# Sample attention scores of a hybrid decoder step: key blocks ordered across four batches, products in four column groups, eight key buffers of two pages

## The chip, the cores and the metric

The kernel runs on one NeuronCore of one Trainium2 chip. The core has five engines with their own instruction streams: PE (matrix products and transposes), DVE (vector work), ACT (scalar functions and copies), POOL (here it issues DMAs) and SP (it only issues DMAs). Sixteen DMA engines move the data. The metric is the device time of one execution in microseconds (us); less is better.

## The reference, cut to what matters

One inference step of a decoder layer for a prompt (512 tokens) and a sample group (8 batches of 4 new tokens, 2048 past positions each in a paged cache of 128 rows a page). The change concerns the attention of the sample group alone. Each batch has its own sixteen pages, named by a page table that is only known at run time:

```python
a_all = jnp.concatenate([gather_pages(cache_a), P['a_rows']], axis=1)      # head group A: k_cmp, v_cmp, k_slc, v_slc, two kv heads
w_all = jnp.concatenate([win_buf, P['win_rows']], axis=1)                  # the last 512 rows: window keys and values
...
s_s = jnp.einsum('bktgd,bktnsd->bktgns', qt, k_s) * scale + bias           # selected blocks (the kernel scores all keys, then masks)
s_w = jnp.einsum('btkgd,bskd->btkgs', qg, kw) * scale + pair_bias(rel_w)   # window
...
s = jnp.einsum('bthd,btkd->bthk', q, k_g) * HEAD_DIM ** -0.5 + bias        # head group C: one kv head, 256 best of 2048 keys
p = masked_softmax(s, ...);  o = jnp.einsum('bthk,btkd->bthd', p, v_g)
```

All of it is float32.

## The kernel before

The program is a chain of five phases; each begins when PE, ACT and DVE have all ended the one before. Phase 4 is the sample attention, phase 5 the output projection. Everything below is phase 4.

**Units and steps.** There are three units: u = 0 (head group A, batches 0 to 3), u = 1 (group A, batches 4 to 7) and u = 2 (group C, all eight batches). In a unit each batch owns 32 of the 128 rows of the scores. `STEPS` (L642) gives the order on every engine: head 0, body 0, head 1, turn 0, body 1, head 2, turn 1, body 2, turn 2. A *head* scores the first eight blocks of a unit (for u < 2 the window keys), a *body* the others (32 blocks for u = 0 and 1, 24 for u = 2), a *turn* transposes the softmax output so that it can multiply the values.

**A block.** PE transposes four 128x128 key tiles into PSUM bank 5 or 6 (`kb`, L1652, transposes on L1660), ACT copies the bank to one of four buffers `kT` (`take_k`, L790), and PE multiplies it with 32 query columns (`kmm`, L1664, product on L1673): 512 score columns in the 32 rows of that batch. A block of units 0 and 1 is four pages of one kv head; so each load of four pages (512 KB) feeds two blocks. A block of unit 2 is four pages of 64 KB. Batches come one after the other: all blocks of batch 0, then of batch 1. The product of a block stands behind the transposes of the next.

**Key loads.** SP walks the loads in the same order (`keys`, L1004) into four buffers `kn` of four pages; a load waits until the buffer's former blocks are transposed (`kb_tr`). A page number is taken from registers: `page` (L682) reads the sixteen page numbers of a batch with one load from the page table tile `ptab` (L684, an instruction TENSOR_LOAD in the trace), and only when the batch differs from the last one (`held`). A few register operations (L686) and one DMA a page follow.

**Value loads.** `values(eng, page, m)` fills one of four buffers `vr`: m = 0 to 15 are half batches of group A (8 pages of 128 KB), m = 16 to 23 the eight batches of group C (16 pages of 64 KB). A load waits until the product four before it is done (`pv_b`). POOL issues m = 0 to 15 and the odd ones of 16 to 23; SP issues the even ones of 16 to 23 behind its last key load.

**Value products.** `pv(u, x)` (L1686, products on L1682) works on batch x // 2 of the former unit and is put into the body of the next one, every 5 blocks (body 1) or 4 blocks (body 2). It already uses four column groups. The fifth call in body 2, `pv(1, 4)`, stands behind the 20th of the 24 blocks, and its two halves free the buffers for m = 16 and 17. Turn 2 ends with the eight products of unit 2, one for each of m = 16 to 23.

**Between the steps.** DVE adds biases and finds the maximum in `late` (L844) when a body's scores are done; the next head's scores wait for it (`un_s`), since they go to the same banks. In bodies 0 and 1 DVE also works off rounds of a top-k over 2080 columns, ahead of `late`. Body 0 starts when `early` (L806) has read the window scores of head 0, for which twelve bias loads must be in.

Of the kernel before, what the change touches and what calls it, by code (L numbers as in the profile page):

```python
# [38 lines left out]
P = 128  # L39
# [4 lines left out]
DB, DT = 8, 4  # L44
# [4 lines left out]
NPG = PAST // PAGE  # L49
NPOOL = 5 * DB * NPG // 4  # L50
HD = 128
AH, KVH, G = 8, 2, 4
# [12 lines left out]
NKR, NVR = 4, 4  # L65
# [125 lines left out]
def build(nc, I, O):  # L191
# [3 lines left out]
    with ExitStack() as ctx:  # L195
# [139 lines left out]
        keep, _ = region(apos[0] + 6 * 1024)  # L335
# [42 lines left out]
        kn = [at_(f"kn{i}", P, 1024) for i in range(NKR)]  # L378
        kT = [at_(f"kT{i}", P, 512) for i in range(4)]
# [9 lines left out]
        assert tpos[0] <= apos[0] + 6 * 1024  # L389
# [110 lines left out]
        vh_in = [sem(f"vh_in{i}") for i in range(2)]  # L500
        kk_in = [sem(f"kk_in{i}") for i in range(NKR)]
# [113 lines left out]
        sblocks, kloads = [], []  # L615
# [12 lines left out]
        kkneed, kc_ = [], [0] * NKR  # L628
        for m, (k_, _, _) in enumerate(kloads):
            kc_[m % NKR] += 16 * k_  # L630
            kkneed.append(kc_[m % NKR])
        vneed, vc_ = [], [0] * NVR
        for m in range(24):
            if m < 16 or m % 2:
                vc_[m % NVR] += 16 * (8 if m < 16 else 16)
                vneed.append((vr_in[m % NVR], vc_[m % NVR]))
            else:
                vneed.append((vh_in[m % NVR // 2], 16 * NPG * (m // 4 - 3)))
# [61 lines left out]
        def values(eng, page, m):  # L700
# [3 lines left out]
            slot, s = vr[m % NVR], vneed[m][0]  # L704
# [85 lines left out]
        def take_k(eng, copy, n, gt, s):  # L790

            eng.wait_ge(kb_tr, gt + 1)
            if n >= 4:
                eng.wait_ge(kb_mm, 32 + n - 3)
            copy(kT[n % 4][:, :], bank[5 + gt % 2][:, :]).then_inc(s, 1)  # L795
# [99 lines left out]
        def _(sp):  # L895
# [108 lines left out]
            def keys(step, u):  # L1004
                for m, (_, last, (lu, kind, b, q)) in enumerate(kloads):
                    if last not in blocks_of(step, u):
                        continue
                    if m >= NKR:
                        sp.wait_ge(kb_tr, kb_gt[kloads[m - NKR][1]] + 1)
                    slot, s = kn[m % NKR], kk_in[m % NKR]  # L1010
                    if kind == "win":
                        sp.dma_start(v3(slot, "p (i c) -> p i c", c=256), sw[b, :, 0, :, :].rearrange("(i p) h c -> p i (h c)", p=P)).then_inc(s, 16)
                    for i in range(4 if kind != "win" else 0):
                        r = page(b, 4 * q + i)
                        if kind == "slc":
                            sp.dma_start(slot[:, i * 256:(i + 1) * 256], ca[bass.ds(r, 1), :, 2, :, :].rearrange("a p h c -> (a p) (h c)")).then_inc(s, 16)
                        else:
# [14 lines left out]
            for m in range(16, 24, 2):  # L1032
                values(sp, page, m)
# [18 lines left out]
        def _(pool):  # L1052
# [110 lines left out]
            for m in [*range(16), *range(17, 24, 2)]:  # L1163
                values(pool, page, m)
# [10 lines left out]
        def _(pe):  # L1175
# [476 lines left out]
            def kb(n):  # L1652

                nonlocal gt
                u, kind, b, q, k, m = sblocks[n]
                pe.wait_ge(kk_in[m % NKR], kkneed[m])
                kturn(gt)
                w = 256 if u < 2 else P
# [65 lines left out]
            for step, u in STEPS:  # L1724
# [997 lines left out]
```

## Time and profile before

| what | value |
|---|---|
| median of 3 runs | 2112.82 us (2109.31 to 2113.4) |
| the profiled execution: its own time | 2106.33 us |
| its span, first to last instruction | 2104.6 us |
| PE, DVE, ACT, POOL busy | 1905.7, 939.8, 563.4, 183.4 us |
| the scores' transposes (L1660) and products (L1673) on PE | 79.5 and 124.9 us |

The span is what the profiler saw between the first and the last instruction; the time lies 1.7 us around it. Busy times of matrix products overlap a little in the trace, since products are pipelined; the distance between two starts is the better price. Phase 4 lies between about 1562 and 1879 us of the span.

### The profile page before, as it was taken

The page shows a single profiled execution, that of the slowest core. Times are in us where ns is not written, and L with a number is a line of the kernel's source. Part 1 is how long each engine was busy: PE and PEld are TensorE (multiplying, and loading weights), DVE is VectorE, ACT ScalarE, POOL GpSimd, SP SyncE. Part 2 cuts the span into 40 slices and gives each one's busy share as a digit, 9 for nine tenths or more (in the row PEclk, how much of TensorE's full clock was granted, in tenths as well). Part 3 has the DMA queues.
Part 4 walks back from the last instruction along what each step waited for, and adds up shares of the span by engine and source line. Part 5 has one row for each costly group of instructions (what it writes and reads, how often), then busy time and mean ns, then how long its engine had stood idle before and what let it go on. Part 6 is the DMA issues. An engine that isn't in the chain of part 4 may idle for free.

```text
span 2104.6 us, 36109 instructions
## 1 busy us (share of the span) xinstructions
PE 1905.7 (91%) x14415; PEld 1620.3 (77%) x14415; DVE 939.8 (45%) x1799; ACT 563.4 (27%) x1117; POOL 183.4 (9%) x338
## 2 busy tenths in 40 slices
PE   5999999999989989578999999889978798869997
PEld 3899999999978878457999999667743333349997
DVE  3122223122442566213888774648758472123331
ACT  2223233124332222123222222034433332231110
POOL 1000000000000001000000000100021043430000
PEclk9999999999989999779999999869999899859999
DMA  8986687724123312243533333650026466672331
GB/s 249 291 223 181 187 241 208 206 90 125 45 66 99 97 59 80 71 130 108 183 110 81 81 102 96 222 186 1 1 80 210 140 218 206 195 218 79 123 123 43
DMA packets 305426, 286.99 MB, mean 136 GB/s; under 512 B 40613, under 2 KB 291990, under 8 KB 303581
## 3 DMA queue, kind: packets, MB, share of 16 engines
q1 hardware_dynamic: 288555, 229.22, 37.6%
q0 software_dynamic: 16704, 55.48, 8.0%
q8 instruction: 114, 1.87, 0.4%
q14 instruction: 53, 0.43, 0.1%
HBM read 268.28 MB, written 29.14 MB: 141 GB/s over the span
## 4 chain that ended last, share of the span: by engine, by line
PE 82%; DMA 4%; DVE 4%; SPq 4%; issue 3%; ACT 1%; ACTq 0%; POOL 0%; POOLq 0%; DVEq 0%
PE bank L1484 6%; PE bank L1486 6%; PE bank L1485 6%; PE bank L1275 6%; PE bank L1277 6%; PE bank L1276 6%; PE bank L1673 5%; PE bank L1809 3%; PE bank L1811 3%; PE bank L1810 3%; PE bank L1525 3%; PE bank L1660 3%; PE bank L1257 3%; PE bank L1526 3%; PE bank L1527 2%
## 5 line engine op out<-in xcount | busy, mean ns | idle before, releaser
L1484 PE MATMUL bank<-h_lo,hw_hi 128*128 128x272 f32 x1024 | 308.4, 301 | 7.6 <-DVE vN L2435 6.7
L1486 PE MATMUL bank<-h_hi,hw_hi 128*128 128x272 f32 x1024 | 298.9, 292 | 0.0
L1485 PE MATMUL bank<-h_hi,hw_lo 128*128 128x272 f32 x1024 | 297.6, 291 | 0.0
L1275 PE MATMUL bank<-w1hi,xl 128*127 128x256 f32 x1024 | 296.5, 290 | 0.0
L1277 PE MATMUL bank<-w1hi,xh 128*127 128x256 f32 x1024 | 289.0, 282 | 0.0
L1276 PE MATMUL bank<-w1lo,xh 128*127 128x256 f32 x1024 | 288.9, 282 | 0.0
L2215 DVE TENSOR_TENSOR xl<-bank,xh 128x512 fp32r<-128x512 f32 x128 | 82.6, 686 | 303.9 <-ACT xh L1881 303.8
L1484 PEld LDWEIGHTS bank<-h_lo,hw_hi 128*128 128x128 f32 x1024 | 195.9, 191 | 19.4 <-issue 11.4
L1485 PEld LDWEIGHTS bank<-h_hi,hw_lo 128*128 128x128 f32 x1024 | 196.2, 192 | 1.5 <-issue 1.0
L1486 PEld LDWEIGHTS bank<-h_hi,hw_hi 128*128 128x128 f32 x1024 | 195.5, 191 | 0.0
L1276 PEld LDWEIGHTS bank<-w1lo,xh 128*127 128x127 f32 x1024 | 193.9, 189 | 0.4
L1275 PEld LDWEIGHTS bank<-w1hi,xl 128*127 128x127 f32 x1024 | 193.4, 189 | 0.5
L1277 PEld LDWEIGHTS bank<-w1hi,xh 128*127 128x127 f32 x1024 | 193.4, 189 | 0.0
L1809 PE MATMUL bank<-mix_lo,wo_hi 128*128 128x272 f32 x512 | 150.4, 294 | 5.8 <-DVE mix_lo L2661 5.8
L2353 DVE TENSOR_TENSOR hw_lo<-hw_raw,hw_hi 128x1024 fp32r<-128x1024 f32 x64 | 78.2, 1222 | 166.7 <-ACT hw_hi L1999 144.4
L1811 PE MATMUL bank<-mix_hi,wo_hi 128*128 128x272 f32 x512 | 149.2, 291 | 0.0
L1810 PE MATMUL bank<-mix_hi,wo_lo 128*128 128x272 f32 x512 | 148.3, 290 | 0.0
L1660 PEld LDWEIGHTS bank<-con,kn 128*128 128x128 f32 x448 | 53.2, 154 | 121.8 <-issue 88.9
L1525 PE MATMUL bank<-pw_hi,h_lo 128*128 128x256 f32 x448 | 131.0, 292 | 0.0
L1526 PE MATMUL bank<-pw_lo,h_hi 128*128 128x256 f32 x448 | 128.1, 286 | 0.0
L1527 PE MATMUL bank<-pw_hi,h_hi 128*128 128x256 f32 x448 | 127.2, 284 | 0.0
L1673 PE MATMUL bank<-kT,zq 128*32 128x512 f32 x224 | 124.9, 645 | 2.3 <-ACT kT L795 2.3
(405 smaller groups left out, 3438.8 us busy)
## 6 DMA issues: line engine op xcount, KB each, us to landing
wa<-in_w_ada_dram SPq DMA_DIRECT2D x24, 2048.0 KB, 9.0
xnat<-in_cache_a_kv_dram SPq DMA_DIRECT2D x256, 128.0 KB, 4.3
hw_raw<-in_w_in_dram SPq DMA_DIRECT2D x64, 512.0 KB, 3.9
pw_raw<-in_w_in_dram SPq DMA_DIRECT2D x16, 1024.0 KB, 6.8
vr<-in_cache_a_kv_dram POOLq DMA_DIRECT2D x128, 128.0 KB, 3.7
kn<-in_cache_a_kv_dram SPq DMA_DIRECT2D x128, 128.0 KB, 2.3
wo<-in_w_out_dram SPq DMA_DIRECT2D x8, 2048.0 KB, 11.7
w1S<-in_a_cmp_w_dram SPq DMA_DIRECT2D x8, 1024.0 KB, 8.1
```

The source lines that it names most:

```text
L1275: mm(o, x4l[:, h, s, a:a + NCS], w1hi[:, cols], start=at, stop=False, skip_group_check=True)
L1276: mm(o, x4h[:, h, s, a:a + NCS], w1lo[:, cols], start=False, stop=False, skip_group_check=True)
L1277: last = mm(o, x4h[:, h, s, a:a + NCS], w1hi[:, cols], start=False, stop=end, skip_group_check=True)
L1484: mm(o, wh, hl[:, k, tc], start=(k == 0), stop=False)
L1485: mm(o, wl, hh[:, k, tc], start=False, stop=False)
L1486: last = mm(o, wh, hh[:, k, tc], start=False, stop=(k == KD - 1))
L1525: mm(o, hl[:, k, tc], wh, start=(k == 0), stop=False)
L1526: mm(o, hh[:, k, tc], wl, start=False, stop=False)
L1673: mm(bank[q][r:r + 32, :], lhs, kT[n % 4][:, :], start=st_, stop=sp_, tile_position=(0, r)).then_inc(kb_mm, 1)
L1809: mm(o, wh[:, k, :], ml[:, k, cols], start=(k == 0), stop=False)
L1810: mm(o, wl[:, k, :], mh[:, k, cols], start=False, stop=False)
L1811: last = mm(o, wh[:, k, :], mh[:, k, cols], start=False, stop=(k == KD - 1))
```

## The change

Blocks and loads are the same thing now: a block is two pages of both kv heads (units 0 and 1; for the windows half a window) or four pages (unit 2), and each block has its own load into one of eight buffers `kn` of half the size. The same bytes are loaded, and as many pages and transposes are worked on. The order of the blocks is turned: four consecutive blocks are the same key range of four batches. `kmm` then issues the products of four blocks together, in four column groups of 32, once the transposes of the next two blocks stand ahead of it. For units 0 and 1 a product has 256 columns instead of 512, and there are two for each block (one for each kv head). `kT` has eight buffers. Two neighbouring blocks share a load semaphore, so that each waits until both are in. All value loads are issued by POOL; SP issues none. Some tiles move to other addresses to make room.

```diff
-NKR, NVR = 4, 4
+NKR, NKT, NVR = 8, 8, 4
...
-        kn = [at_(f"kn{i}", P, 1024) for i in range(NKR)]
-        kT = [at_(f"kT{i}", P, 512) for i in range(4)]
+        kn = [at_(f"kn{i}", P, 512) for i in range(NKR)]
+        kT = [at_(f"kT{i}", P, 512) for i in range(NKT)]
...
-            for kind, nq in (("win", 1), ("slc", 4)):
-                for b in range(4 * u, 4 * u + 4):
-                    for q in range(nq):
-                        for k in range(KVH):
-                            sblocks.append((u, kind, b, q, k, len(kloads)))
-                        kloads.append((1 if kind == "win" else 4, len(sblocks) - 1, (u, kind, b, q)))
-        for b in range(DB):
-            for q in range(4):
-                sblocks.append((2, "c", b, q, 0, len(kloads)))
-                kloads.append((4, len(sblocks) - 1, (2, "c", b, q)))
+            sblocks += [(u, "win", b, f) for f in range(2) for b in range(4 * u, 4 * u + 4)]
+            sblocks += [(u, "slc", b, f) for f in range(8) for b in range(4 * u, 4 * u + 4)]
+        sblocks += [(2, "c", b, f) for f in range(4) for e in range(2) for b in range(e, DB, 2)]
+        NDMA = {"win": 1, "slc": 2, "c": 4}
...
-                for m, (_, last, (lu, kind, b, q)) in enumerate(kloads):
-                    if last not in blocks_of(step, u):
-                        continue
-                    if m >= NKR:
-                        sp.wait_ge(kb_tr, kb_gt[kloads[m - NKR][1]] + 1)
-                    slot, s = kn[m % NKR], kk_in[m % NKR]
+                for n in blocks_of(step, u):
+                    _, kind, b, f = sblocks[n]
+                    if n >= NKR:
+                        sp.wait_ge(kb_tr, kb_gt[n - NKR] + 1)
+                    slot, s = kn[n % NKR], kk_in[n % NKR // 2]
...
+                    elif kind == "slc":
+                        for i in range(2):
+                            r = page(b, 2 * f + i)
...
+                    else:
+                        for i in range(4):
+                            r = page(b, 4 * f + i)
...
-            for m in range(16, 24, 2):
-                values(sp, page, m)
...
-            for m in [*range(16), *range(17, 24, 2)]:
+            for m in range(24):
                 values(pool, page, m)
...
-                mm(bank[q][r:r + 32, :], lhs, kT[n % 4][:, :], start=st_, stop=sp_, tile_position=(0, r)).then_inc(kb_mm, 1)
+                turn_taken(pe, kb_gt[n0 + 3])
+                for k in range(2):
+                    for n in range(n0, n0 + 4):
+                        u, kind, b, f = sblocks[n]
+                        if u < 2:
+                            r, c0 = 32 * (b % 4), f % 2 * 256
+                            last = mm(bank[f // 2][r:r + 32, c0:c0 + 256], zq[:, u * 256 + k * P + r:u * 256 + k * P + r + 32], kT[n % NKT][:, k * 256:(k + 1) * 256],
+                                      start=(k == 0), stop=(k == 1), tile_position=(0, r))
+                        elif k == 1:
+                            r = 32 * (b // 2)
+                            last = mm(bank[f][r:r + 32, :], zq[:, 512 + 32 * b:512 + 32 * b + 32], kT[n % NKT][:, :],
+                                      start=(b % 2 == 0), stop=(b % 2 == 1), tile_position=(0, r))
...
-                    if n > ns[0]:
-                        kmm(n - 1)
                     y = n - ns[0] + 1
+                    if y > 4 and y % 4 == 2:
+                        kmm(n - 5)
```

On SP, the first key loads of body 0 stood like this before (`kn0` and `kn1` are buffers, ISA is a register operation of L686; the line numbers of the changed file are some ten lower):

```order
L684 TENSOR_LOAD ptab_76
L686 ISA
L1016 DMA kn0_220<-in_cache_a_kv_dram 128x256
L686 ISA
L1016 DMA kn0_220<-in_cache_a_kv_dram 128x256
L686 ISA
L1016 DMA kn0_220<-in_cache_a_kv_dram 128x256
L686 ISA
L1016 DMA kn0_220<-in_cache_a_kv_dram 128x256
L686 ISA
L1016 DMA kn1_221<-in_cache_a_kv_dram 128x256
```

and stand like this in the changed kernel:

```order
L675 TENSOR_LOAD ptab_76
L677 ISA
L1006 DMA kn0_220<-in_cache_a_kv_dram 128x256
L677 ISA
L1006 DMA kn0_220<-in_cache_a_kv_dram 128x256
L675 TENSOR_LOAD ptab_76
L677 ISA
L1006 DMA kn1_221<-in_cache_a_kv_dram 128x256
L677 ISA
L1006 DMA kn1_221<-in_cache_a_kv_dram 128x256
L675 TENSOR_LOAD ptab_76
```

A load of the page registers stood ahead of sixteen page loads in units 0 and 1 and stands ahead of every two now; in unit 2 it stood ahead of sixteen and stands ahead of every four.

On POOL, at the end of phase 4, the values of group C stood like this before (buffers `vr1` and `vr3` alone, since SP filled `vr0` and `vr2`):

```order
L712 DMA vr1_229<-in_cache_c_kv_dram 128x128
L684 TENSOR_LOAD ptab_76
L686 ISA
L712 DMA vr3_231<-in_cache_c_kv_dram 128x128
L686 ISA
L712 DMA vr3_231<-in_cache_c_kv_dram 128x128
```

and stand like this in the changed kernel:

```order
L703 DMA vr0_236<-in_cache_c_kv_dram 128x128
L675 TENSOR_LOAD ptab_76
L677 ISA
L703 DMA vr1_237<-in_cache_c_kv_dram 128x128
L677 ISA
L703 DMA vr1_237<-in_cache_c_kv_dram 128x128
```

POOL's stream has all eight batches one after the other now, 128 page loads in place of 64, and SP's has none of them behind the keys.

On PE, the start of body 0 in the changed kernel (`zq` holds the queries; L1650 are the transposes, L1662 the products):

```order
L1650 MATMUL bank5<-con_49,kn4_224 128x128 x4
L1650 MATMUL bank6<-con_49,kn5_225 128x128 x4
L1662 MATMUL bank0<-kT0_228,zq_64 32x256
L1662 MATMUL bank0<-kT1_229,zq_64 32x256
L1662 MATMUL bank0<-kT2_230,zq_64 32x256
L1662 MATMUL bank0<-kT3_231,zq_64 32x256
L1662 MATMUL bank0<-kT0_228,zq_64 32x256
L1662 MATMUL bank0<-kT1_229,zq_64 32x256
```

Before, one product of 512 columns stood behind each four transposes; eight products of 256 columns stand together now, behind the transposes of blocks 5 and 6 of the step.

## Rows read from the trace of the kernel before

**Rows 1.** First line of the page.

```profile
span 2104.6 us, 36109 instructions
```

**Rows 2.** Timeline of PE in body 0: start, length, engine, line, operation.

```profile
1604.44 0.66 PE L1660 MATMUL bank<-con,kn 128*128 128x128 f32 x4
1605.03 1.04 PE L1673 MATMUL bank<-kT,zq 128*32 128x512 f32 x2
1606.01 0.66 PE L1660 MATMUL bank<-con,kn 128*128 128x128 f32 x4
```

**Rows 3.** Timeline of PE: where steps begin or end; in brackets idle time before.

```profile
1592.73 1.94 PE L1660 MATMUL bank<-con,kn 128*128 128x128 f32 x8 [6.16 <-issue]
...
1644.63 0.63 PE L1770 MATMUL bank<-ksN,zq 128*128 128x32 f32 x4
1652.87 1.97 PE L1660 MATMUL bank<-con,kn 128*128 128x128 f32 x8 [7.61 <-DVE us L856]
...
1669.57 0.63 PE L1770 MATMUL bank<-ksN,zq 128*128 128x32 f32 x4
...
1677.89 1.10 PE L1660 MATMUL bank<-con,kn 128*128 128x128 f32 x8 [3.30 <-issue]
...
1740.84 0.63 PE L1770 MATMUL bank<-ksN,zq 128*128 128x32 f32 x4
...
1749.01 1.97 PE L1660 MATMUL bank<-con,kn 128*128 128x128 f32 x8 [4.28 <-DVE us L856]
...
1765.62 0.62 PE L1695 MATMUL bank<-con,opart 128*128 128x16 f32 x4
...
1770.69 1.09 PE L1660 MATMUL bank<-con,kn 128*128 128x128 f32 x8 [0.77 <-DVE pT L786]
...
1829.22 0.41 PE L1780 MATMUL bank<-ksN,qf 128*128 128x32 f32 x2
...
1875.43 0.60 PE L1682 MATMUL bank<-cvN,pT 32*32 32x128 f32 x2 [4.04 <-DMA vr<-in_cache_c_kv_dram]
...
1884.71 0.57 PE L1809 MATMUL bank<-mix_lo,wo_hi 128*128 128x272 f32 x1 [5.83 <-DVE mix_lo L2661]
```

**Rows 4.** Timeline of DVE: the first step of `late` in bodies 0 and 1.

```profile
1645.37 2.48 DVE L848 TENSOR_TENSOR sS<-bank,sbias 128x512 f32<-128x512 f32 x4 [7.67 <-PE bank L1770]
...
1741.51 2.48 DVE L848 TENSOR_TENSOR sS<-bank,sbias 128x512 f32<-128x512 f32 x4 [14.80 <-PE bank L1770]
```

**Rows 5.** Chain that ended last, in body 2: start, length, engine, line.

```profile
1792.13 0.98 SPq L684
...
1818.26 3.26 PE bank L1682 x46
```

**Rows 6.** Line L684 by engine: durations in ns, shortest, median, longest.

```profile
L684 SPq TENSOR_LOAD <-ptab x68: 967/974/1177, 11.0 to 1855.2; - x68
L684 POOLq TENSOR_LOAD <-ptab x12: 1048/1056/1294, 1562.6 to 1858.4; - x12
```

**Rows 7.** Timeline of SP, indexer keys of phase 2: four pages for each register load.

```profile
859.68 11.17 SPq L698 DMA_DIRECT2D ixn<-in_cache_c_kidx_dram  x16
```

**Rows 8.** Timeline of SP, key loads of body 2.

```profile
1763.22 59.63 SPq L1018 DMA_DIRECT2D kn<-in_cache_c_kv_dram  x96
```

**Rows 9.** Timeline of SP, sixteen pages of one batch (m = 16).

```profile
1824.06 8.33 SPq L712 DMA_DIRECT2D vr<-in_cache_c_kv_dram  x16
```

**Rows 10.** Timeline of POOL: a new batch in head 0, and one batch (m = 19).

```profile
1575.37 0.54 POOL L708 DMA_DIRECT2D vr<-in_cache_a_kv_dram  x1 [1.17 <-issue]
...
1834.64 9.52 POOL L712 DMA_DIRECT2D vr<-in_cache_c_kv_dram  x16 [1.58 <-issue]
```

**Rows 11.** DMA issues: count, size of one, median us to landing.

```profile
kn<-in_cache_c_kv_dram SPq DMA_DIRECT2D x128, 64.0 KB, 2.7
...
vr<-in_cache_c_kv_dram POOLq DMA_DIRECT2D x64, 64.0 KB, 2.4
```

**Rows 12.** Windows, turn 2: length, busy of PE, PEld, DVE, ACT, POOL, clock, DMA.

```profile
1838.70:1878.90 40.20, 26.48 (x305) 18.88 (x305) 2.03 (x10) 3.56 (x11) 22.53 (x43) 0.54 0.64 191
```

More of the change, by code:

```diff
@@ L499, in build @@
         vr_in = [sem(f"vr_in{i}") for i in range(NVR)]
-        vh_in = [sem(f"vh_in{i}") for i in range(2)]
-        kk_in = [sem(f"kk_in{i}") for i in range(NKR)]
+        kk_in = [sem(f"kk_in{i}") for i in range(4)]
         wv_in = sem("wv_in")
@@ L611, in build @@
         NUA = QT * AH
-        sblocks, kloads = [], []
+        sblocks = []
         for u in range(2):
-            for kind, nq in (("win", 1), ("slc", 4)):
-                for b in range(4 * u, 4 * u + 4):
-                    for q in range(nq):
-                        for k in range(KVH):
-                            sblocks.append((u, kind, b, q, k, len(kloads)))
-                        kloads.append((1 if kind == "win" else 4, len(sblocks) - 1, (u, kind, b, q)))
-        for b in range(DB):
-            for q in range(4):
-                sblocks.append((2, "c", b, q, 0, len(kloads)))
-                kloads.append((4, len(sblocks) - 1, (2, "c", b, q)))
-        IXB = (0, 2, 4, 6, 1, 3, 5, 7)
[L628 to L631, printed above, removed]
+            sblocks += [(u, "win", b, f) for f in range(2) for b in range(4 * u, 4 * u + 4)]
+            sblocks += [(u, "slc", b, f) for f in range(8) for b in range(4 * u, 4 * u + 4)]
+        sblocks += [(2, "c", b, f) for f in range(4) for e in range(2) for b in range(e, DB, 2)]
+        NDMA = {"win": 1, "slc": 2, "c": 4}
+        IXB = (0, 2, 4, 6, 1, 3, 5, 7)
+        kkneed, kc_ = [], [0] * 4
+        for n, (_, kind, _, _) in enumerate(sblocks):
+            kc_[n % NKR // 2] += 16 * NDMA[kind]
+            kkneed.append(kc_[n % NKR // 2])
+        kkneed = [kkneed[n | 1] for n in range(len(sblocks))]
         vneed, vc_ = [], [0] * NVR
         for m in range(24):
[L634 to L638, printed above, removed]
+            vc_[m % NVR] += 16 * (8 if m < 16 else 16)
+            vneed.append((vr_in[m % NVR], vc_[m % NVR]))
         NBLK = (40, 40, 32)
@@ L792, in take_k @@
             eng.wait_ge(kb_tr, gt + 1)
-            if n >= 4:
-                eng.wait_ge(kb_mm, 32 + n - 3)
-            copy(kT[n % 4][:, :], bank[5 + gt % 2][:, :]).then_inc(s, 1)
+            if n >= NKT:
+                eng.wait_ge(kb_mm, 32 + n - NKT + 1)
+            copy(kT[n % NKT][:, :], bank[5 + gt % 2][:, :]).then_inc(s, 1)
         def unit_exps(eng, A, u, when):
@@ L1004, in keys @@
             def keys(step, u):
-                for m, (_, last, (lu, kind, b, q)) in enumerate(kloads):
-                    if last not in blocks_of(step, u):
-                        continue
-                    if m >= NKR:
-                        sp.wait_ge(kb_tr, kb_gt[kloads[m - NKR][1]] + 1)
-                    slot, s = kn[m % NKR], kk_in[m % NKR]
+                for n in blocks_of(step, u):
[3 more added lines that the diff above has]
+                    slot, s = kn[n % NKR], kk_in[n % NKR // 2]
                     if kind == "win":
[L1012 to L1015, printed above, removed]
+                        sp.dma_start(v3(slot, "p (i c) -> p i c", c=256), sw[b, 256 * f:256 * f + 256, 0, :, :].rearrange("(i p) h c -> p i (h c)", p=P)).then_inc(s, 16)
+                    elif kind == "slc":
+                        for i in range(2):
+                            r = page(b, 2 * f + i)
                             sp.dma_start(slot[:, i * 256:(i + 1) * 256], ca[bass.ds(r, 1), :, 2, :, :].rearrange("a p h c -> (a p) (h c)")).then_inc(s, 16)
-                        else:
+                    else:
+                        for i in range(4):
+                            r = page(b, 4 * f + i)
                             sp.dma_start(slot[:, i * P:(i + 1) * P], cc[bass.ds(r, 1), :, 0, :].rearrange("a p c -> (a p) c")).then_inc(s, 16)
@@ L1761, in _ @@
                         pv(u - 1, y // every - 1)
-                kmm(ns[-1])
+                kmm(ns[-1] - 3)
                 if u < 2:
```

26 lines of the change are left out of this document (10 added, 16 removed).

## The prediction

> **What bounds the kernel now.** I began with the page for the span [rows 1] and then read the stretch of phase 4 step by step on PE, since the change touches nothing else. In body 0 the reader sees a steady beat: four transposes, 0.59 us from start to start, then one product, 0.98 us, so 1.57 us a block with no idle time between [rows 2]. There PE sets the pace, and the products are the larger part of it. The next view is where the steps begin and end on PE [rows 3]; between a body's last product (L1770) and the next head lie 7.6 to 8.2 us in which DVE finds the maximum, and the change leaves these alone. DVE's own timeline says how much a faster body can give: it was idle for 7.67 us ahead of `late` in body 0 and for 14.80 us in body 1 [rows 4], since its top-k rounds fill the rest. More than that cannot be won in these two bodies as long as body 0 starts where it does. In body 2 it is no longer PE alone: SP needed 59.63 us for the 96 key loads of 24 blocks [rows 8], and the chain that ended last goes through SP's register load itself [rows 5]. The end of the phase waits for values: the last product of turn 2 began at 1875.43, behind a wait of 4.04 us for its DMA [rows 3], and phase 5 follows 9.28 us later.
>
> **What the change removes on PE.** The value products already run in four column groups, and the chain shows 46 of their passes of 256 columns in 3.26 us, 0.071 us each [rows 5]. In units 0 and 1 four blocks now need 16 such passes (two products each of two passes), 1.14 us, where they needed 4 x 0.98 = 3.92. With the transposes a group of four costs 4 x 0.59 + 1.14 = 3.5 us in place of 6.28, or 0.88 us a block. In unit 2 it is 8 passes of 512 columns, about the same 1.1 us. If PE alone counted, that would be some 0.69 us for each of 112 blocks, 77 us, capped in bodies 0 and 1 by DVE as above. ACT's copies are as many as before and fit under this.
>
> **What it adds on SP.** The blocks now change the batch at every step, and `page` keeps one batch only. So there is a register load ahead of each block of units 0, 1 (64) and 2 (32): 96 where there were 16. One costs 0.974 us on SP [rows 6]. What it costs in a row of loads is seen where the indexer keys do just that, four pages for each load: 16 pages and three loads between them took 11.17 us [rows 7], and 16 pages without any load 8.33 us [rows 9]. That is (8.33 - 0.33) / 15 = 0.533 us a page (0.33 is the last DMA itself) and (11.17 - 8.33) / 3 = 0.947 us a load: nothing of it is hidden. A block of units 0 and 1 thus costs SP 2 x 0.533 + 0.947 = 2.01 us, a block of unit 2 4 x 0.533 + 0.947 = 3.08. Check on before: 96 x 0.533 + 5 x 0.947 = 55.9 of the 59.63 us [rows 8]. Against PE's 0.88 us SP becomes the bound of every body, and it is slower than the old beat of 1.57. Eight buffers hold the same bytes as four did, so SP can run eight blocks ahead while PE waits for DVE, and no further.
>
> **The steps, one after the other.** After SP's last issue of a step I add 2.7 us to landing [rows 11], and 4.0 us for the two transposes of the last pair, one copy and the last group (3.1 at PE's pace in rows 2; 5.3 if PE has the lower clock; I take the middle).
> Body 0 starts at 1592.73 as before: it waits for DVE and that for the bias loads, which the four more window issues on SP delay by 2 us at most. Its first eight blocks are loaded by then; the ninth needs a buffer that is freed some 1.1 us later, and 24 x 2.01 = 48.2 us bring SP to 1642.0 and the last score to 1648.7, where it was 1644.63: 4.1 later.
> Head 1 follows 8.24 us behind, at 1657.0. Its eight blocks (half of them at the slow clock of a PE that had been idle: 8 x 1.1 + 2.9) take 11.7 us, not 16.7; the window loads, 4 MB with `win_v`, are in by then. End 1668.7, 0.9 earlier than 1669.57.
> Turn 0 is unchanged (8.32 us): body 1 at 1677.0. From 1678.0 SP has 24 blocks, to 1726.2; last score 1732.9, 7.9 earlier than 1740.84. PE's own work there, 32 x 0.88 and 10 us of value products, is covered.
> Head 2 could start at 1741.1, but SP needs 8 x 3.08 = 24.6 us after 1726.2, so it ends at 1757.5, 8.1 earlier than 1765.62. Turn 1 keeps its 5.07 us.
> Body 2: SP goes on at once, from 1753.0 behind the four `win_v` issues (2.2 us). The 20th block is issued 61.6 us later, at 1814.6, landed at 1817.3 and transposed at 1818.9. There `pv(1, 4)` starts, at 1818.26 before. **Up to here the gain on PE and the price on SP cancel.**
>
> **The tail.** `pv(1, 4)` frees the buffer of m = 16 after about two thirds of its 3.26 us, at 1821.1, and POOL starts loading with a gap of 1.17 us [rows 10], at 1822.3. Before, SP and POOL shared the eight batches, four each. Now POOL issues all: 9.52 us for sixteen pages and 1.17 us for a new batch [rows 10], so 8 x 9.52 + 7 x 1.17 = 84.4 us; with a short pause now and then I take 85.5. None of its waits holds it up: the products free the buffers faster. The last page is issued at 1907.8 and lands 2.4 us after its start [rows 11], at 1909.7, where the last product began at 1875.43: 34.3 us later. PE then does one product after each batch of POOL and waits. The 9.28 us to phase 5, and phase 5, are as before, since its first weights are asked for earlier than now.
> What rows 10 and 11 show is an issue bound: the bytes of a page are there 2.4 us after its issue, and still the batch takes 9.52 us. The Trainium skill, "DMA: Bandwidth & Descriptors", section "Issuing engines are not separate DMA queues", says that issuing from several engines saves only the time to initiate a DMA, which is usually small relative to the DMA itself. By that the move to POOL would be nearly free, and the sum 34 us less; with pages of 64 KB the rows speak against "small".
>
> **The sum.** +0.6 to the start of `pv(1, 4)`, +33.7 in the tail: 34.3. On the profiled execution's 2106.33 us that gives 2140.6. The three runs have a median 6.5 us above that execution, so 2147. Unknown: a register load between 0.8 and 1.1 us (76 of them stand in the chain, but DVE and the eight buffers take some back: 9 us down, 8 up), POOL's batch between 9.52 + 1.06 [rows 6] and 11.2 us (2 down, 4 up), the end of each step between 3.1 and 5.3 us (3 either way). The likeliest case's own range is 2138 to 2158.
>
> **The rivals.**
> *The register loads vanish* (faster). If SP read the registers while its former DMAs are being issued, a block would cost it 1.07 or 2.13 us, and PE and DVE would set the pace: body 0 ends 7.7 us earlier [rows 4], head 1 takes 5 less, body 1 gains DVE's 14.8, head 2 another 5, body 2 some 16 to the 20th block. That is 49 us, less 34 for the tail: 15 faster, 2091, or 2098 on the scale of the runs. It decides from a load of some 0.5 us downwards: then the 76 loads in the chain give back the tail. For it speaks only that nothing in rows 2 limits PE; against it rows 7 and 9. 5 in 100.
> *The tail costs nothing*, because the values lie in their buffers before the products need them. Then only the end of body 2 counts: SP ends at 1826.9, the last score at 1833.6 against 1829.22, 4.4 later: 2110.7, or 2117 (2105 if the waits for values in turn 2 go as well). It is what the rule of the Trainium skill's "DMA: Bandwidth & Descriptors" above would make of the move. Against it stands the wait of 4.04 us with two issuers. 6 in 100.
> *PE loses its clock.* In turn 2, where PE worked 26.48 of 40.2 us with gaps, the granted clock was 0.54, mostly the lower of the levels 1.2 and 2.4 GHz [rows 12]. With PE idle more than half of the time in bodies 0 and 1, it could fall there too; a group of four would take 7.0 us, still under SP's 8.04, but in body 1 the value products (three, 6.5 us each) come on top: 56 + 20 + 2 = 78 us in place of 56. That makes 22 us more, 2169. 8 in 100.
> That the loads come from fewer batches at a time, and so don't change the batch, is excluded by the order of instructions.
>
> **Chances.** 79 in 100 for the forecast, 5, 6 and 8 for the rivals, 2 for others. About 0.2% (4 us) is what the spread of the runs can tell. The first rival is faster; of the second about four fifths is no change and the rest slower; all else is slower: 0.06, 0.05, 0.89. The range 2131 to 2168 leaves out the first two rivals and most of the third, and a little of the forecast's own spread on both sides.
>
> **What would show it.** Right: 96 register loads on SP in phase 4 where there were 20 (16 for keys, 4 for values); 2.0 us from block to block on PE in bodies 0 and 1 and 3.1 in body 2 with DMA of `kn` as releaser; products at about 0.07 us a pass; DVE's idle time ahead of `late` in body 0 some 4 us longer; batches of POOL 10.7 us apart from about 1822 to 1908, and PE waiting for `vr` some 7 us in each of the last products. Wrong: a beat near 0.9 us in the bodies (the first rival), `vr` waits in turn 2 no longer than before (the second), transposes of 1.1 us all through body 1 (the third).

## The result

The changed kernel takes 2158.26 us (median, 2151.68 to 2160.08), the kernel before 2111.34 us in runs on the same chip: a ratio of 1.0217, with a 95% interval of 1.0192 to 1.0242. It is slower, by 46.9 us; forecast were 34.3 us more than before and a time of 2147. The 2158 lie inside the stated range (2131 to 2168), at the upper end of what the prediction gave its likeliest case (2138 to 2158). One run of e5 below, of 4076.65 us, was in a slow state and is left out there.

The profiled execution took 2159.07 us, 52.7 more than the profiled one of before. The page's first line answers [rows 1]:

```profile
span 2157.4 us, 36513 instructions
```

Timeline of PE, where the steps begin or end, in the order of [rows 3] (the line numbers are some ten lower); after the last product of body 1 come the end of head 2, the starts of body 2 and of `pv(1, 4)`, the last product and phase 5:

```profile
1599.54 1.94 PE L1650 MATMUL bank<-con,kn 128*128 128x128 f32 x8 [6.74 <-issue]
1657.13 1.07 PE L1766 MATMUL bank<-ksN,zq 128*128 128x32 f32 x4
1665.81 1.97 PE L1650 MATMUL bank<-con,kn 128*128 128x128 f32 x8 [7.61 <-DVE us L847]
1676.51 0.63 PE L1766 MATMUL bank<-ksN,zq 128*128 128x32 f32 x4
1684.84 4.79 PE L1650 MATMUL bank<-con,kn 128*128 128x128 f32 x20 [3.31 <-issue]
1744.53 0.63 PE L1766 MATMUL bank<-ksN,zq 128*128 128x32 f32 x4
1769.88 1.04 PE L1691 MATMUL bank<-con,opart 128*128 128x16 f32 x4
1776.79 1.09 PE L1650 MATMUL bank<-con,kn 128*128 128x128 f32 x8 [0.77 <-DVE pT L777]
1832.92 0.62 PE L1678 MATMUL bank<-vN,pT 32*32 32x256 f32 x4
1927.54 0.60 PE L1678 MATMUL bank<-cvN,pT 32*32 32x128 f32 x2 [7.54 <-DMA vr<-in_cache_c_kv_dram]
1936.84 0.56 PE L1805 MATMUL bank<-mix_lo,wo_hi 128*128 128x272 f32 x1 [5.84 <-DVE mix_lo L2657]
```

Phase 4 itself begins 7.8 us later in this execution (SP's first key load of the phase at 1570.36, before at 1562.55). That is not the change: e4 below, whose code is that of before up to the value loads of group C, begins phase 4 at 1568.77, and variants of the changed kernel that differ from it only within phase 4 begin it between 1565.72 (e11) and 1572.28 us (e5). With the 7.8 us taken off, the steps moved like this against before:

| point on PE | forecast | measured |
|---|---|---|
| end of body 0 | +4.1 | +4.7 |
| end of head 1 | -0.9 | -0.9 |
| end of body 1 | -7.9 | -4.1 |
| end of head 2 | -8.1 | -3.5 |
| start of `pv(1, 4)` | +0.6 | +6.9 |
| last product of turn 2 | +34.3 | +44.3 |

So 7 of the 44.3 us have come by `pv(1, 4)`, and 37.4 come behind it.

The first mechanism is seen in the chain that ended last, in body 2 (start, length, engine, line):

```profile
1798.20 0.97 SPq L675
1799.34 0.33 SPq L1010
1799.87 0.33 SPq L1010
1800.39 0.33 SPq L1010
1800.91 0.33 SPq L1010
1801.30 0.97 SPq L675
...
1804.39 0.97 SPq L675
```

From one register load to the next lie 3.10 and 3.09 us, and SP waits for nothing between: four page issues and the load, end to end, 3.08 by the forecast. For the blocks of body 0 it is 2.07 us, 2.01 by the forecast (two loads of the same chain):

```profile
1583.65 0.97 SPq L675
1585.72 0.97 SPq L675
```

In body 1 six loads in a row, from 1726.2 to 1736.6, stand 2.08 us apart. In body 0 the products of a group of four blocks stand 8.03 us apart on average, four intervals from 1617.49 to 1649.59, and PE waits for `kn` ahead of the transposes (timeline of PE in body 0):

```profile
1610.93 1.07 PE L1662 MATMUL bank<-kT,zq 128*32 128x256 f32 x16
...
1617.49 1.58 PE L1662 MATMUL bank<-kT,zq 128*32 128x256 f32 x16
...
1633.28 1.93 PE L1662 MATMUL bank<-kT,zq 128*32 128x256 f32 x16
...
1640.17 1.97 PE L1650 MATMUL bank<-con,kn 128*128 128x128 f32 x8 [3.11 <-DMA kn<-in_cache_a_kv_dram]
...
1649.59 1.94 PE L1662 MATMUL bank<-kT,zq 128*32 128x256 f32 x16
```

Line L675 by engine answers [rows 6]: 76 more register loads on SP (96 for keys where there were 16, and none for values where there were four), four more on POOL, each as long as before:

```profile
L675 SPq TENSOR_LOAD <-ptab x144: 967/972/1465, 11.3 to 1839.8; - x144
L675 POOLq TENSOR_LOAD <-ptab x16: 1050/1060/1288, 1570.4 to 1914.7; - x16
```

The second is seen in POOL's timeline of the tail, first the start of m = 16, then two whole batches (as in [rows 10]):

```profile
1838.71 8.32 POOL L703 DMA_DIRECT2D vr<-in_cache_c_kv_dram  x14 [15.50 <-PE bank L1678]
...
1882.05 9.52 POOL L703 DMA_DIRECT2D vr<-in_cache_c_kv_dram  x16 [1.17 <-issue]
...
1916.37 9.52 POOL L703 DMA_DIRECT2D vr<-in_cache_c_kv_dram  x16 [1.15 <-issue]
```

From 1838.71 to the last product at 1927.54 are 88.8 us. The DMA issues of that stretch (count, size of one, median us to landing) say, as [rows 11] did, that a page is soon there after its issue; the next page's issue is what is late:

```profile
vr<-in_cache_c_kv_dram POOLq DMA_DIRECT2D x128, 64.0 KB, 2.1
```

PE's waits in phase 4 (in total, times, longest) show both prices, values first:

```profile
PE bank L1678 <- DMA vr<-in_cache_c_kv_dram: 42.3, 6, 9.6
PE bank L1650 <- DMA kn<-in_cache_c_kv_dram: 32.3, 12, 4.9
PE bank L1650 <- DMA kn<-in_cache_a_kv_dram: 29.8, 16, 5.3
```

### The profile page after: what moved, and what is told of

Its sections match the earlier page's. It is cut to its first block, busy times and chain, and to the rows that moved or that the text cites. A ratio compares the mean times of both kernels' runs of the same rounds, so it can differ in the third digit from the quotient of the medians.

```text
span 2157.4 us, 36513 instructions
## 1 busy us (share of the span) xinstructions
PE 1863.7 (86%) x14575; PEld 1646.5 (76%) x14575; DVE 939.8 (44%) x1799; ACT 561.0 (26%) x1117; POOL 217.3 (10%) x402
## 4 chain that ended last, share of the span: by engine, by line
PE 76%; SPq 6%; DMA 6%; issue 5%; DVE 4%; ACT 1%; ACTq 0%; POOLq 0%; POOL 0%; DVEq 0%
PE bank L1474 6%; PE bank L1475 6%; PE bank L1476 6%; PE bank L1265 6%; PE bank L1267 6%; PE bank L1266 6%; PE bank L1805 3%; PE bank L1807 3%; PE bank L1806 3%; PE bank L1515 3%; PE bank L1247 3%; PE bank L1516 2%; PE bank L1517 2%; DMA kn<-in_cache_a_kv_dram 2%; PE bank L1650 2%
## 5 line engine op out<-in xcount | busy, mean ns | idle before, releaser
L1650 PE MATMUL bank<-con,kn 128*128 128x128 f32 x448 | 88.0, 359 | 98.8 <-DMA kn<-in_cache_c_kv_dram 32.3
L1650 PEld LDWEIGHTS bank<-con,kn 128*128 128x128 f32 x448 | 69.0, 185 | 127.7 <-DMA kn<-in_cache_c_kv_dram 42.7
```

Of the source, the lines that this page charges most:

```text
L1650: last = tr(bank[5 + gt % 2][:, to * P:(to + 1) * P], kn[n % NKR][:, i * P:(i + 1) * P], ident)
```

## The experiments

Each time is a median, each ratio is to the kernel before, run on the same chip among them, with a 95% interval.

**e1: the even batches of values back on SP.** The changed kernel, with POOL's loop shortened and SP's put back behind its last key load:

```diff
-            for m in range(24):
+            for m in [*range(16), *range(17, 24, 2)]:
...
+            for m in range(16, 24, 2):
+                values(sp, page, m)
```

> The changed kernel, but the value loads of group C are shared as before: SP issues the even batches behind its keys, POOL the odd ones. Theory of the prediction (POOL's issue of eight batches makes the tail): in the changed kernel 94.6 us lie between the start of pv(1, 4) and the last product of turn 2, before 57.3; sharing gives most of that back, all but the 9 to 12 us by which SP reaches its value loads later than before. Expected 2118 to 2128 us where the kernel before has 2111, and waits for values in turn 2 of 4 us at most each. Rival A (the transfers or their landing make the tail, not their issue): no change, 2150 to 2160. Rival B (the key stages are the larger loss): under 15 us faster than the changed kernel.

Measured: 2126.11 us, 1.0081 (1.0053 to 1.0110). The waits for values in turn 2 are three, of 4 to 5 us where at most 4 were expected, and from `pv(1, 4)` (1836.17) to the last product are 64.1 us, where the changed kernel took 94.6:

```profile
1882.39 0.60 PE L1685 MATMUL bank<-cvN,pT 32*32 32x128 f32 x2 [4.79 <-DMA vr<-in_cache_c_kv_dram]
...
1900.31 0.60 PE L1685 MATMUL bank<-cvN,pT 32*32 32x128 f32 x2 [4.54 <-DMA vr<-in_cache_c_kv_dram]
```

So the second issuer is worth 29 to 32 us (the ratios, the medians).

**e4: the move of the values alone.** The kernel before, with all of `range(24)` on POOL and none on SP.

> The kernel before with one part of the change alone: POOL issues the values of all eight batches of group C. Keys, blocks and products are the old ones. Theory of the prediction: pv(1, 4) starts where it did, and the tail behind it is as long as in the changed kernel, 93 to 96 us in place of 57; expected 2145 to 2150 us. Rival A (the transfers make the tail): 2108 to 2116. If the tail is longer only because products of turn 2 come at another time in the changed kernel, it lies between, about 2125.

Measured: 2142.88 us, 1.0172 (1.0141 to 1.0203), a little less than expected. `pv(1, 4)` began at 1820.62, the last product 93.7 us later, behind the same waits as in the changed kernel:

```profile
1903.56 0.60 PE L1680 MATMUL bank<-cvN,pT 32*32 32x128 f32 x2 [9.70 <-DMA vr<-in_cache_c_kv_dram]
1914.36 0.60 PE L1680 MATMUL bank<-cvN,pT 32*32 32x128 f32 x2 [7.79 <-DMA vr<-in_cache_c_kv_dram]
```

In the kernel before these were 57.25 us, from this start (timeline of PE) to 1875.43 [rows 3]:

```profile
1818.18 0.62 PE L1682 MATMUL bank<-vN,pT 32*32 32x256 f32 x4
```

The tail needs nothing else of the change. The rival that it costs nothing falls.

**e2: one register load for four blocks.** The changed kernel, with the four batches' numbers read together:

```diff
-                            r = page(b, 2 * f + i)
+                        if n % 4 == 0:
+                            sp.load(kregs[0:8], ptab3[:, b:b + 4, 2 * f:2 * f + 2])
+                            r = sp.snap(kregs[2 * (n % 4) + i], ...)
...
-                            r = page(b, 4 * f + i)
+                        if n % 4 == 0:
+                            sp.load(kregs, ptab3[:, b:DB:2, 4 * f:4 * f + 4])
+                            r = sp.snap(kregs[4 * (n % 4) + i], ...)
```

> The changed kernel, but one register load reads the page numbers of four blocks (8 or 16 registers), so there are 24 loads for keys and not 96; the values stay on POOL alone. Theory of the prediction (register loads pace the key stages): a block costs SP 1.07 + 0.24 = 1.3 us in units 0 and 1 and 2.13 + 0.24 = 2.4 in unit 2; body 0 then ends with DVE's top-k (7 us earlier than in the kernel before), pv(1, 4) starts about 40 us earlier than in the kernel before, and with the long tail behind it the time is 2104 to 2116 us. Rival (PE's lower clock or the prefetch of eight blocks paces the key stages, not the register loads): less than 10 us faster than the changed kernel, 2148 to 2158.

Measured: 2118.25 us, 1.0044 (1.0023 to 1.0064): 36 to 40 us less than the changed kernel, and 2 us over the upper end of what was expected. One reason is in the loads of the two lines (shortest, median, longest in ns): four pairs of numbers cost 1.72 us, four fours 1.04.

```profile
L1008 SPq TENSOR_LOAD <-ptab x16: 1704/1716/1741, 1582.2 to 1710.4; - x16
```

```profile
L1014 SPq TENSOR_LOAD <-ptab x8: 1031/1035/1050, 1716.4 to 1793.0; - x8
```

**e3: both.** e1 and e2 together.

> The changed kernel with both: one register load for four blocks, and group C's values shared by SP and POOL. If the two causes are separate and explain the loss, their gains add: about 36 us under the one with group loads alone, 2066 to 2080 us, faster than the kernel before by 1.5 to 2%. If one hides the other (values again wait for POOL, or DVE and PE set the pace anyway), it stays within 15 us of the better of the two.

Measured: 2082.51 us, 0.9873 (0.9843 to 0.9902), again 2 us over the expectation, but 1.3% faster than the kernel before. The two costs add: 40 and 32 us apart by the medians, 76 together.

**e9: e3 without the column groups.** e3, with each block's products by themselves, behind the next block's transposes:

```diff
-            def kmm(n0):
+            def kmm(n):
-                turn_taken(pe, kb_gt[n0 + 3])
-                for k in range(2):
-                    for n in range(n0, n0 + 4):
-                        u, kind, b, f = sblocks[n]
+                turn_taken(pe, kb_gt[n])
+                u, kind, b, f = sblocks[n]
...
+                    if n > ns[0]:
+                        kmm(n - 1)
-                    if y > 4 and y % 4 == 2:
-                        kmm(n - 5)
```

> The version with both costs of the change removed (one register load for four blocks, even c-value batches back on SP; 2082.5 us), but with the score products of each block by themselves, behind the next block's transposes, in place of four column groups at once. Theory A, the column groups are what TensorE gains (a block from 1.57 us to 0.88): with them gone TensorE sets body 1 again (52 us in that version, 63 in the kernel before), the two heads of 8 blocks lose 5.5 us each of which some lies beside waits, and body 0, which SP mostly sets, loses little: 12 to 28 us more, 2094 to 2110. Theory B, SP's issue sets the pace even with the grouped register loads, so the column groups bring nothing, and the 26 us that the version gains on the kernel before come from the eight small buffers: 2080 to 2088.

Measured: 2104.47 us, 0.9954 (0.9934 to 0.9973). Body 1, from its first transpose to its last score product, in e3 and then in e9 (timelines of PE):

```profile
1672.07 2.30 PE L1664 MATMUL bank<-con,kn 128*128 128x128 f32 x9 [3.31 <-issue]
...
1723.98 0.63 PE L1780 MATMUL bank<-ksN,zq 128*128 128x32 f32 x4
```

```profile
1683.70 1.94 PE L1664 MATMUL bank<-con,kn 128*128 128x128 f32 x8 [3.30 <-issue]
...
1747.65 0.63 PE L1778 MATMUL bank<-ksN,zq 128*128 128x32 f32 x4
```

51.9 us with column groups, 64.0 without, 62.9 in the kernel before [rows 3]. The groups bring 17 to 22 us where SP lets PE use them. The 0.5% by which e9 is still faster than the kernel before belong to the rest of that version (order of the blocks, buffers, register loads), which was not taken apart.

**e5: the changed kernel without the column groups.** The same edit on the changed kernel.

> The changed kernel (2158 us) with the score products of each block by themselves, behind the next block's transposes, so TensorE's gain is given back and SP's register load for each block stays. Theory A, SP sets the pace at 2.01 us a block in units 0 and 1 and 3.08 in unit 2, and TensorE's 1.57 hide behind it: only the heads, whose eight blocks are loaded ahead, lose up to 0.69 us a block (5.5 us a head, of which the blocks of lead give part back): 2156 to 2168. Theory B, the column groups bring the same wherever they stand (22 us, as in the version with both costs removed): 2176 to 2184.

Measured: 2161.04 us (three runs, 2156.43 to 2168.69), 1.0239 (1.0212 to 1.0266), 3 to 5 us more than the changed kernel, with intervals that overlap. The same edit costs 17 to 22 us in e3: in the changed kernel most of the groups' gain lay behind SP. In the traces body 1 takes 64.5 us here (1691.15 to 1755.68) and 59.7 in the changed kernel, where e9 and e3 are 12 us apart.

**e8: the register loads alone, in the kernel before.**

```diff
+                    if kind != "win":
+                        sp.load(kregs, ptab[0:1, b * NPG:(b + 1) * NPG])
...
-                        r = page(b, 4 * q + i)
+                        r = sp.snap(kregs[4 * q + i], ...)
```

> The kernel before (2108 us) with a register load of its own ahead of each of the 64 key loads of four pages, 48 more than it had, and nothing else changed. Theory A, a register load costs 0.95 us on SP and counts only where SP sets the pace: in units 0 and 1 SP's key load takes 2.13 + 0.95 = 3.08 us for two blocks, and TensorE takes 3.14 for them, so nothing shows there; in unit 2 a key load serves one block, SP goes from about 2.45 us a block (59.63 us for 96 pages, 24 blocks) to 3.08, so 0.65 to 0.71 for 24 to 32 blocks, 15 to 23 us: 2120 to 2132, all of it after the third head. Theory B, the price falls on the path wherever the load stands: 48 x 0.95 = 46 us: 2148 to 2158. Theory C, register loads run beside the transfers that are under way and cost nothing: 2105 to 2112.

Measured: 2131.15 us, 1.0095 (1.0070 to 1.0121): 18 to 20 us more. Phase 4 began 6.7 us later than in the trace of before; with that taken off, body 1 ended 2.7 us earlier than there (1744.86 against 1740.84), so the 24 loads added up to there cost nothing. The key loads of body 2 took 76.13 us, 59.63 before [rows 8]:

```profile
1769.77 76.13 SPq L1022 DMA_DIRECT2D kn<-in_cache_c_kv_dram  x96
```

A register load costs what SP has no slack for: nothing while PE needs 3.14 us for the two blocks of a load, and in body 2, where a load serves one block, 16.5 us for 18 more, 0.92 each.

**e7 and e11: smaller loads.** The changed kernel, with each load reading only what its block needs (e7: two numbers in units 0 and 1, four in unit 2), or always an aligned four (e11):

```diff
-                            r = page(b, 2 * f + i)
+                        sp.load(kregs[0:2], ptab[0:1, b * NPG + 2 * f:b * NPG + 2 * f + 2])                # e7
+                        sp.load(kregs, ptab[0:1, b * NPG + 2 * (f - f % 2):b * NPG + 2 * (f - f % 2) + 4])  # e11
```

> The changed kernel with each register load reading only the two or four page numbers of its block, not the sixteen of its batch. Theory A, what a register load costs SP is a fixed price of some 0.95 us, whatever it reads: 2152 to 2162, and the loads show 0.9 us or more each. Theory B, the price goes by the registers that it fills (0.97 us for sixteen, so 0.12 for two and 0.24 for four): SP's block falls from 2.01 to 1.19 us and from 3.08 to 2.37, and the time comes near the kernel with one load for four blocks: 2112 to 2124.

> The changed kernel with a register load of four page numbers (an aligned four, of which a block of units 0 and 1 uses two) for each block, where the run before read two numbers there (2124.7 us). That run's loads took 0.472 us for two numbers and 0.297 for four. Theory A, the price goes by the run of numbers, and two cost more than four: the loads of units 0 and 1 show some 0.30 us, SP's block falls by 0.175 us, 11 us over 64 blocks, of which waits take part: 2113 to 2121. Theory B, the 0.472 us belong to the place in the program (the loads between SP's transfers of two pages), not to the numbers read: 2122 to 2128, and the loads still show 0.47 us.

Measured: e7 2124.65 us, 1.0056 (1.0036 to 1.0075); e11 2113.84 us, 1.0027 (1.0014 to 1.0039). The time of e7 is 0.65 us over what its second theory gives, but its loads show neither theory's price; the time and the loads of e11 are as by its first. The loads of units 0 and 1 in e7, those of unit 2 in e7, and those of units 0 and 1 in e11:

```profile
L1006 SPq TENSOR_LOAD <-ptab x64: 462/472/497, 1582.2 to 1715.9; - x64
```

```profile
L1011 SPq TENSOR_LOAD <-ptab x32: 294/297/314, 1717.5 to 1805.4; - x32
```

```profile
L1006 SPq TENSOR_LOAD <-ptab x64: 293/297/316, 1575.0 to 1703.3; - x64
```

The price goes by what is read, not by the instruction, and two numbers cost more than four. With e11 alone 40 to 44 of the 47 us are gone, although every block still has its load.

**e10: e3 with fours only.** One load of sixteen numbers (four batches, four numbers each) for eight blocks of units 0 and 1.

> The version with both costs removed (2082.5 us), with the page numbers of units 0 and 1 read sixteen at a time for eight blocks (four batches, four numbers each), not eight at a time for four blocks (four batches, two numbers each). The traces show 1.72 us for the load of four pairs and 1.04 us for the load of four fours, so SP's share falls from 0.43 to 0.13 us a block, 19 us over the 64 blocks. Theory A, SP still sets bodies 0 and 1 there (TensorE waits 20 us for these keys): 6 to 16 us faster: 2066 to 2077. Theory B, TensorE, the landing of a pair and the eight buffers set them: 2078 to 2086.

Measured: 2077.28 us, 0.9848 (0.9827 to 0.9869), 5 us less than e3, at the edge between the two expectations. The new bound shows ahead of head 1 (timeline of PE): it waits 12.48 us for DVE, not 7.61, since DVE's top-k rounds are not done when body 0 is.

```profile
1652.65 1.97 PE L1664 MATMUL bank<-con,kn 128*128 128x128 f32 x8 [12.48 <-DVE us L851]
```

This is the fastest version that was run, 1.5% under the kernel before.

**e6: six key buffers** (`NKR = 6`, three semaphores).

> The changed kernel with six key buffers where it has eight (all else as changed; 2158 us). Theory A, SP sets the bodies by its own issue, register load and two or four pages a block, and loses time of its own only where the buffers stop it while TensorE is held at a head, a turn or value products: two buffers less take two blocks of lead away at the starts of the bodies and in the value products of body 1, at 2.01 us a block in units 0 and 1 and 3.08 in unit 2, so 4 to 14 us more: 2162 to 2172. If the 3.8 us that body 1 took beyond the forecast came from such stops, that body grows here by 3 us or more. Theory B, the extra time of body 1 and turn 1 is TensorE's lower granted clock and the depth of the buffers has no part in it: 2155 to 2161, and body 1 as long as before within 1.5 us.

Measured: 2163.43 us, 1.0243 (1.0222 to 1.0264), some 5 us more than the changed kernel, within what the first theory expects. But body 1 is only 1.6 us longer (1679.46 to 1749.11 between the ends of head 1 and body 1, 69.65 against 68.02), and 5 us come in body 0, whose end moves from 1657.13 to 1661.30 with a phase that began 1.2 earlier. There the trace has the stop: ahead of the load at 1601.82 SP stands still for 5.69 us, with eight buffers for 0.94 (at 1600.66). For body 1 this decides nothing.

**e12: few value products in body 1.** The changed kernel, which leaves out 19 of the 23 value products of each batch of unit 0, so that the sums of that unit are not complete:

```diff
+                    if u == 0:
+                        products = [products[7 + i] for i in (0, 7, 8, 15)]
```

> The changed kernel (2158 us) with only four of the 23 value products of each batch of unit 0, so that TensorE's stops for them in body 1 fall from 3.5 to 6.3 us each to about 1 us; the four keep the waits and the releases of the value buffers, and the rest of the sums is left out. It asks why SP's 48 issues for the last 24 blocks of body 1 took 51.5 us where 24 blocks at 2.01 are 48.2. Theory A, the eight buffers stop SP while TensorE does value products: the issues take 48.2 to 49.3 us, body 1 is 3 us or more shorter than 59.7 from its first transpose to its last score product, and the time is 2151 to 2156. Theory B, the extra time is not from the value products (keys that land later while POOL's value loads are under way, or the start of the body): the issues take 50.8 us or more, the body shortens by less than 1.5 us, and the time is 2156 to 2161.

Measured: 2156.74 us, 1.0213 (1.0181 to 1.0244). SP's last 48 issues in body 1 took 49.34 us, in the changed kernel 51.48 (timelines of SP, e12 and then the changed kernel):

```profile
1686.57 49.34 SPq L1006 DMA_DIRECT2D kn<-in_cache_a_kv_dram  x48
```

```profile
1687.11 51.48 SPq L1006 DMA_DIRECT2D kn<-in_cache_a_kv_dram  x48
```

Yet body 1 did not get shorter (60.8 us, 59.7 with all products): PE then waited 4.79 and 1.76 us for the last keys. The body and the time are as by the second theory. The issues are near what the first one gives, but not for its reason: in both runs SP's register loads follow each other every 2.07 us while PE works on values. The 2.1 us lie in single page issues. This is the line of the changed kernel in that stretch (shortest, median, longest in ns):

```profile
L1006 SPq DMA_DIRECT2D kn<-in_cache_a_kv_dram x48: 332/333/1585, 1687.1 to 1738.3; - x48
```

It has two such long issues, of 1.58 us (at 1689.71) and 1.42 us (at 1724.74); the longest in e12 took 0.82 (at 1691.24). Each of the three falls beside a 16 KB transfer of the queue q8, of the kind "instruction" (from 1689.62, 1724.63 and 1690.75). Other such transfers pass without a long issue (at 1628.74), and that they are the cause is not shown.

## Why the prediction came out as it did

**The two mechanisms are shown.** SP's register load ahead of each block sets the bodies: e2, e7 and e11 make the load cheaper and take 34 to 44 us away; e5 gives back PE's gain and loses 3 to 5, hardly clear of the scatter of its runs. The one issuer sets the tail: e4 adds it to the kernel before (35 to 36 us), e1 takes it away (29 to 32 us). Together they are the whole loss and the gain besides (e3).

**Step by step.** PE's beat with column groups was priced right: 16 passes in 1.07 us at the full clock (1.14 forecast). SP's blocks of 2.01 and 3.08 us are there, as 2.07 and 3.10. Body 0 (+4.7) and head 1 (-0.9) came within 0.6 us, in part by luck: with the 7.8 us taken off, body 0 began 1.0 us earlier than forecast, and SP's 24 blocks in it took 50.1 us, not 48.2 (1600.66 to 1650.74); head 1 began 1.0 us later and took 10.7 us, not 11.7. DVE's idle time ahead of `late` in body 0 grew from 7.67 us [rows 4] to 13.79, 6 and not 4:

```profile
1658.30 2.48 DVE L839 TENSOR_TENSOR sS<-bank,sbias 128x512 f32<-128x512 f32 x4 [13.79 <-PE bank L1766]
```

**Mis-sized: "24 x 2.01" us in body 1.** Forecast was that SP goes on without a stop, from 1678.0 to 1726.2. With the 7.8 us added it began as forecast (its load at 1685.95) and ended 4.6 us later (1738.59). A period of 2.07 us in place of 2.01 makes 1.4 of these over 24 blocks, the two long page issues (e12) make 2.3, shorter pauses the rest. The view of waits is easily misread here: it lists 14 waits of SP's loads for buffers in this body, 10.0 us in all. But all save the first of these loads start 0.05 us after the page issue ahead of them, as loads without a wait do, so these waits cost nothing; the first, of 2 us at the start of the body, is in the forecast.

From there the delay goes on into body 2. With 0.6 us more in the keys of head 2, SP starts that body 5.2 us behind the forecast (its load at 1765.98; forecast 1753.0 and the 7.8). The 20 blocks up to `pv(1, 4)` took 64.5 us, not 61.6: 3.10 us each, and again single long issues (1.29 us at 1807.11) and pauses. Landing and transposes took 2.4 us, not 4.3. That makes 6.2 us at the start of `pv(1, 4)`. What makes single issues long is open. In body 1 POOL's value loads run beside SP's keys, and between 1696 and 1705 the keys took 3.8 us to land where 2.2 is the median of all. That these transfers hold them back was not tried by itself and stays open.

**Mis-sized: the way from `pv(1, 4)` to POOL's start.** It took 5.8 us, 3.4 were forecast. The 3.26 us of the chain [rows 5] were those of a PE at full clock; here the product lasted 5.0 us, and the granted clock was 0.60 in its first 3.7 us. In e5, where the same product lasted 3.3 us (from 1844.01), the way took 4.2 us, so the slower product is 1.6 us of the difference. The eight batches took 88.8 us from the first issue to the last product, 87.4 by the forecast; one pause of 2.04 us stands in them.

The three pieces, 6.2, 2.4 and 1.4 us, are the 10 us between 34.3 and 44.3. Turn 1 took 6.9 us, not 5.07, but that was PE's time alone: the keys were later still, and PE waited 2.81 us for them at 1780.69.

**The rivals.** *The register loads vanish*: no; yet its rule that with loads below some 0.5 us the bodies give back the tail is nearly what e7 and e11 found: with loads of 0.47 and 0.30 us they are 0.6 and 0.3% slower than the kernel before. *The tail costs nothing*: no. The Trainium skill, "DMA: Bandwidth & Descriptors", section "Issuing engines are not separate DMA queues", calls the time to initiate a DMA usually small relative to the DMA. Here the traces disagree: a page of 64 KB takes POOL 0.6 us to issue (9.52 for sixteen) and lands in 2.1, and two issuers are 29 to 36 us faster than one (e1, e4). *PE loses its clock*: it was lower in body 1 where PE had become idle (windows: length, busy of PE, PEld, DVE, ACT, POOL, clock, DMA; the start of `pv(1, 4)`, the rest of turn 2, body 1), but the keys were later still, and the rival's 78 us for body 1 did not come (59.7). What did come of it is the slower `pv(1, 4)` above. In turn 2 it was near the lower of its levels, as it was before [rows 12]:

```profile
1832.90:1836.60 3.70, 3.70 (x37) 1.82 (x40) 0.00 (x0) 0.76 (x2) 0.00 (x0) 0.60 0.33 92
...
1850.00:1927.50 77.50, 30.89 (x318) 20.05 (x317) 8.72 (x21) 5.66 (x13) 60.23 (x112) 0.52 0.41 123
1684.84:1744.53 59.69, 45.26 (x408) 27.69 (x409) 47.52 (x47) 20.03 (x39) 24.89 (x47) 0.81 0.64 206
```

## What to carry to other kernels

When an order of work is changed for one engine, walk the same order on the queue that feeds it: a cache of one entry (`held`) that hit three times in four here missed every time afterwards, and its price, hidden before, became the beat. Price a queue's issue by its whole period (load and DMAs, end to end) and compare it with the consumer's new beat, not with the old one. The gain may still be there: with the numbers read in fours for eight blocks and two issuers for the values the same order of blocks and the same column groups are 1.5% faster than the kernel before (e10), and e9 against e3 puts the groups' own part at 17 to 22 us, about 1%.

## What the runs showed of the hardware that was not expected

- The price of SP's register load goes by what it reads and how it lies: 0.297 us for four neighbouring numbers, 0.97 for sixteen, 1.04 for four separate fours, but 0.47 for a pair and 1.72 for four separate pairs. An estimate from these five that comes within 0.05 us of each is 0.07 us and then 0.23 for each four or 0.41 for each pair; reading numbers that are not needed made it cheaper.
- In body 1 PE was busy for less of the time and had a lower clock: before, 62.48 of 62.95 us at a granted clock of 0.97 (windows, as above), now 45.26 of 59.69 us at 0.81, in e12 37.78 of 60.80 us at 0.76. A batch's value products took 5.8 us there at worst, 3.3 at best. In this kernel that mostly hid behind SP's keys.

```profile
1677.89:1740.84 62.95, 62.48 (x345) 24.42 (x345) 47.53 (x47) 20.70 (x39) 25.79 (x48) 0.97 0.66 213
```
